# A two-layer hybrid decoder step on one core: the samples' state updates of twenty heads taken from TensorE to VectorE, and one more buffer for the first modulation weights

## The reference

```python
mod = silu(c) @ w_ada + b_ada
shift, scale, gate = split(mod, 3)
h = rmsnorm(x) * (1 + scale) + shift
cols = h @ w_in                       # q, k, v of each head, z, two gates
o = each head group's recurrence      # with a state of 128x128 per head and sample
y = x + gate * ((headnorm(o) * silu(z)) @ w_out)
```

## Time and profile before

| | us |
|---|---|
| median of three runs | 2323.64 |
| profiled execution | 2323.17 |
| its span | 2321.6 |
| TensorE busy | 2266.9 |
| VectorE busy | 1283.8 |
| ScalarE busy | 738.1 |
| POOL busy | 907.0 |

### The profile page before, as it was taken

One profiled execution on the slowest core, in us unless ns is written; L12 is line 12 of the kernel. 1 busy time (PEld: TensorE's weight loads), 2 busy tenths in 40 slices (PEclk: granted clock), 3 DMA queues, 4 the chain that ended last, 5 costly groups with the idle time before them and its releaser, 6 DMA issues.

```text
span 2321.6 us, 50275 instructions
## 1 busy us (share of the span) xinstructions
PE 2266.9 (98%) x21347; PEld 2161.7 (93%) x21347; DVE 1283.8 (55%) x2506; ACT 738.1 (32%) x1175; POOL 907.0 (39%) x668
## 2 busy tenths in 40 slices
PE   4899999999999999999999999999999999999998
PEld 3799999999999999998879999999999999999998
DVE  6346666677776344442126566567777753435444
ACT  2143322333333333421124333233333433334111
POOL 3033333333334343554333333333333443346542
PEclk9999999999999999999999999999999999999999
DMA  9952222554453333366775222244453333323332
GB/s 400 378 185 93 93 94 97 162 164 160 159 178 99 116 99 117 103 219 239 267 268 201 77 93 93 91 161 156 166 164 107 112 101 124 113 86 109 121 112 106
DMA packets 153647, 347.21 MB, mean 150 GB/s; under 512 B 14816, under 2 KB 85408, under 8 KB 127544
## 3 DMA queue, kind: packets, MB, share of 16 engines
q1 hardware_dynamic: 153424, 344.01, 43.1%
HBM read 312.07 MB, written 32.09 MB: 148 GB/s over the span
## 4 chain that ended last, share of the span: by engine, by line
PE 89%; DVE 4%; DMA 2%; DVEq 1%; POOL 1%; ACT 1%; issue 1%; SPq 0%; ACTq 0%; POOLq 0%
PE pj L685 72%; PE mx L691 3%; PE mx L1028 2%; DMA rows<-in_ada_first 1%; PE mx L1054 1%; PE mx L1042 1%; PE mx L778 1%; PE mx L744 1%; POOL wlo L653 1%; DMA spare_piece<-in_ada_first 1%; DVE t L1501 1%; PE pj L1150 1%; PE mx L1006 1%; PE mx L1056 1%; PE mx L1046 1%; PE mx L937 1%
## 5 line engine op out<-in xcount | busy, mean ns | idle before, releaser
L685 PE MATMUL pj<-hh,whi 128*128 128x260 f32 x4928 | 1418.0, 288 | 4.7 <-DVE hl L1501 3.2
L685 PE MATMUL pj<-hl,whi 128*128 128x260 f32 x4928 | 1392.8, 283 | 0.0
L685 PE MATMUL pj<-hh,wlo 128*128 128x260 f32 x4928 | 1390.6, 282 | 0.0
L653 POOL TENSOR_TENSOR wlo<-raw,whi 128x512 fp32r<-128x512 f32 x632 | 862.6, 1395 | 1323.5 <-ACT whi L1229 1323.5
L685 PEld LDWEIGHTS pj<-hh,whi 128*128 128x128 f32 x4928 | 928.1, 188 | 52.5 <-issue 46.2
L685 PEld LDWEIGHTS pj<-hl,whi 128*128 128x128 f32 x4928 | 928.5, 188 | 0.0
L685 PEld LDWEIGHTS pj<-hh,wlo 128*128 128x128 f32 x4928 | 928.0, 188 | 0.0
L1229 ACT ACTIVATE whi<-raw 128x2048 fp32r<-128x2048 f32 x158 | 302.9, 1917 | 256.8 <-PE pj L685 186.8
L1229 ACT ACTIVATE xv<-pj 128x260 f32<-128x260 f32 x188 | 64.7, 383 | 380.2 <-PE pj L685 379.9
L1501 DVE SCALAR_TENSOR_TENSOR o<-pj,mod,t 128x260 f32<-128x260 f32 (+1 forms) x56 | 24.6, 480 | 230.1 <-PE pj L685 214.5
L1229 ACT ACTIVATE t<-t 128x520 f32<-128x520 f32 (+1 forms) x126 | 79.2, 629 | 182.1 <-DVEq L1761 132.8
(11 more groups left out here) (290 smaller groups left out, 2283.3 us busy)
## 6 DMA issues: line engine op xcount, KB each, us to landing
raw<-in_w_tiles SPq DMA_DIRECT2D x128, 1024.0 KB, 4.9
raw<-in_wo_tiles SPq DMA_DIRECT2D x32, 1024.0 KB, 5.0
lev<-in_w_ada SPq DMA_DIRECT2D x90, 256.0 KB, 4.6
rows<-in_ada_first SPq DMA_DIRECT2D x22, 1024.0 KB, 21.1
lev<-in_w_ada SPq DMA_DIRECT2D x39, 512.0 KB, 5.7
out<-ss SPq DMA_DIRECT2D x32, 512.0 KB
xv<-in_w_ada SPq DMA_DIRECT2D x25, 512.0 KB, 5.8
y_kept<-o SPq DMA_DIRECT2D x2, 4160.0 KB, 17.9
```

Of the source, the lines that this page charges most:

```text
L653: last = e.tensor_tensor((wlo_third if t == 2 else wlo[:, par, :])[:, cs], w[:, cs], high_of(t)[:, cs].bitcast(F32), ALU.subtract)
L685: last = e.matmul(pj[:, 2 * par + b, 0:HALF], w[:, par, kb * P:(kb + 1) * P], x[:, kb, b * HALF:(b + 1) * HALF], start=(kb == 0 and m == 0 ...
```

## The change

- In the 20 heads that are not mLSTM (8 HGRN2, 12 retention) `sample_rows` and the four 2x256 matmuls of `states_u` are gone, as are ScalarE's copies of `apart` and `sr` and VectorE's `blocks`. Instead ScalarE issues, right after the copy of v and before the next rounding, a DMA of the samples' v (128 partitions x 8 elements) to `v_kept` in DRAM, transposed to 8 rows of 128, so element by element (`keep_v`). SP, at j = 1 of the head, waits for it and loads v_kept into `big`, the same 4 KB for all 128 partitions (512 KB). VectorE multiplies `big` by k and adds it to `ss` (`outer`, two operations of 128x1024), in HGRN2 heads before the wait for `ps["u"]`, in retention heads after "chain".
- ScalarE waits for `v_saved` before it copies vt.
- `states_u` of retention heads (but for g = 0) runs after part 3 instead of 4.
- LOW_FIRST is 2: VectorE makes two remainders of `o` ahead of `ps["u"]` and none later; POOL makes fourteen instead of twelve.
- An eleventh home for the first pieces, made of two halves: z's and zw's buffer (`z_zw`) and a new `gate_bs` that holds gate_b and gate_sum. Its piece is loaded by two DMAs of 512 KB; piece 10, its first, waits for `sq_sum`. The pieces are dealt anew (`piece_slot`), and the last ones stand in another order in TensorE's program.

```diff
@@ -282,8 +286,9 @@
         srow = rows_t[0:NS, 2 * half_h + D:2 * half_h + 2 * D]
-        piece_at = [rows_t[:, kb * TOK:kb * TOK + D] for kb in range(0, 2 * KB, 4)] + [xv[:, 0:D], spare_t[:]]
-        piece_slot = [0, 4, 1, 5, 2, 6, 3, 7, 8, 9, 1, 5, 2, 6, 3, 7, 8, 9, 2, 6, 3, 7, 8, 9, 3, 7, 8, 9, 3, 7, 8, 9]
+        piece_at = [rows_t[:, kb * TOK:kb * TOK + D] for kb in range(0, 2 * KB, 4)] + [xv[:, 0:D], spare_t[:], None]
+        halves_at = (z_zw[:, 0:D // 2], gate_bs[:])
+        piece_slot = [0, 4, 1, 5, 2, 6, 3, 7, 8, 9, 10, 1, 5, 2, 6, 3, 7, 8, 9, 10, 2, 6, 3, 7, 8, 9, 10, 3, 7, 8, 9, 10]
         yrow, ysrow = xrow, srow
...
@@ -422,7 +431,13 @@
                     e.wait_ge(piece_used, earlier[-1] + 1)
-                e.dma_start(at, ada_first[p]).then_inc(piece_in[piece_slot[p]], 16)
+                if at is None:
+                    if p == 10:
+                        e.wait_ge(sq_sum, 1)
+                    for b, half in enumerate(halves_at):
+                        e.dma_start(half, ada_first[p][:, b * D // 2:(b + 1) * D // 2]).then_inc(piece_in[piece_slot[p]], 16)
+                else:
+                    e.dma_start(at, ada_first[p]).then_inc(piece_in[piece_slot[p]], 16)
...
@@ -544,6 +559,11 @@
                             continue
+                        if j == 1 and kind != "ml":
+                            e.wait_ge(v_saved, 16 * (plain_before(g) + 1))
+                            e.wait_ge(head_done, g + 1)
+                            e.wait_ge(ps["score"], scorec(l, h, LEVELS + 1 if kind == "hg" else 1))
+                            e.dma_start(big, v_kept.rearrange("s d -> (s d)").partition_broadcast(P)).then_inc(v_in, 16)
                         if h + 1 < NH:
...
@@ -715,11 +735,14 @@
                     n, pieces = column_block(u)[2:]
-                    e.wait_ge(piece_in[piece_slot[p]], 16 * (loads_of(p) + 1))
+                    e.wait_ge(piece_in[piece_slot[p]], (32 if piece_slot[p] == 10 else 16) * (loads_of(p) + 1))
                     if i == 0 and u >= 2:
                     for x in range(FIRST_K):
-                        w = piece_at[piece_slot[p]].rearrange("p (k j n) -> p k j n", k=FIRST_K, j=4)[:, x]
+                        if piece_slot[p] == 10:
+                            w = halves_at[x // 2].rearrange("p (k j n) -> p k j n", k=FIRST_K // 2, j=4)[:, x % 2]
+                        else:
+                            w = piece_at[piece_slot[p]].rearrange("p (k j n) -> p k j n", k=FIRST_K, j=4)[:, x]
                         for j in range(4):
...
@@ -892,22 +915,22 @@
                     first_piece(24)
+                    first_piece(25)
                     third_block(6)
                     pair_block(9)
-                    first_piece(25)
                     first_piece(26)
+                    first_piece(27)
                     pair_block(10)
                     pair_block(11)
-                    first_piece(27)
                     first_piece(28)
                     first_piece(29)
+                    third_block(8)
                     first_piece(30)
-                    third_block(8)
+                    third_block(9)
                     first_piece(31)
-                    third_block(9)
                     block_columns(7)
...
@@ -992,8 +1016,10 @@
                             v_rows()
-                            k_rows()
-                            sample_rows().then_inc(ps["tr"], 1)
+                            last = k_rows()
+                            if kind == "ml":
+                                last = sample_rows()
+                            last.then_inc(ps["tr"], 1)
...
@@ -1033,17 +1059,18 @@
                             e.wait_ge(vs["a"], g + 1)
-                            e.wait_ge(vs["blk"], g + 1)
                             e.wait_ge(as_["vt"], g + 1)
                             e.wait_ge(as_["kt"], g + 1)
-                            e.wait_ge(as_["sr"], g + 1)
+                            if kind == "ml":
+                                e.wait_ge(vs["blk"], n + 1)
+                                e.wait_ge(as_["sr"], n + 1)
                             w = HD + 1 if kind == "ml" else HD
                                 last = e.matmul(mx[:, c, 0:w], kt[:, c, :], vt[:, c, 0:w], start=True, stop=True)
-                            lhs = sw if kind == "ml" else sr[:, 1, :]
-                            for j in range(4):
-                                r = slice(32 * j, 32 * j + 2)
-                                last = e.matmul(mx[:, j, 256:512], lhs[r, :], big[r, 0:256], start=True, stop=True)
+                            if kind == "ml":
+                                for j in range(4):
+                                    r = slice(32 * j, 32 * j + 2)
+                                    last = e.matmul(mx[:, j, 256:512], sw[r, :], big[r, 0:256], start=True, stop=True)
                             last.then_inc(ps["u"], 1)
...
@@ -1090,7 +1117,7 @@
                             return ({}, {}, {(2, 1): (scores, rows)}), {2: (states_u,), 4: (outputs,), 8: (back,)}
-                        return ({}, {}, {1: (scores, rows), 4: (states_u,), 7: (outputs,)}), {5: (back,)}
+                        return ({}, {}, {1: (scores, rows), 3: (states_u,), 7: (outputs,)}), {5: (back,)}
...
@@ -1353,6 +1380,8 @@
                             last.then_inc(taken, 1)
+                            if kept is not None:
+                                kept()
...
@@ -1365,19 +1394,16 @@
-                            if g:
-                                e.wait_ge(ps["tr"], g)
-                            e.wait_ge(taken, ht(g, 2))
-                            vqk = xv[:, 2 * (PAD + TOK):2 * (PAD + TOK) + 3 * TOK].rearrange("p (m t) -> p m t", m=3)[:, :, T:TOK]
-                            if scaled == "hg":
-                                act(by_four(apart[:, 1:2, :]), by_four(x1[:, PAD + T:PAD + TOK].unsqueeze(1)), ACT.Copy)
-                                last = act(by_four(apart[:, 0:3:2, :]), by_four(vqk[:, 0:3:2, :]), ACT.Copy)
+                            if scaled == "ml":
+                                e.wait_ge(taken, ht(g, 2))
+                                vqk = xv[:, 2 * (PAD + TOK):2 * (PAD + TOK) + 3 * TOK].rearrange("p (m t) -> p m t", m=3)[:, :, T:TOK]
+                                e.wait_ge(vs["qk"], g + 1)
+                                act(by_four(apart[:]), by_four(vqk), ACT.Copy).then_inc(as_["apart"], 1)
+                            e.wait_ge(ps["tr"], g + 1)
+                            if scaled == "ml":
+                                act(sr[0:GR], mx[0:GR, 3, 0:3 * HD].rearrange("p (j d) -> p j d", j=3), ACT.Copy).then_inc(as_["sr"], 1)
                             else:
-                                e.wait_ge(vs["qk"], g + 1)
-                                last = act(by_four(apart[:]), by_four(vqk), ACT.Copy)
-                            last.then_inc(as_["apart"], 1)
-                            e.wait_ge(ps["tr"], g + 1)
-                            act(sr[0:GR], mx[0:GR, 3, 0:3 * HD].rearrange("p (j d) -> p j d", j=3), ACT.Copy).then_inc(as_["sr"], 1)
+                                e.wait_ge(v_saved, 16 * (plain_before(g) + 1))
                             act(vt[:, :, 0:HD], mx[:, 1, :].rearrange("p (c d) -> p c d", c=NC), ACT.Copy).then_inc(as_["vt"], 1)
...
@@ -1387,6 +1413,13 @@
+                        def keep_v():
+
+                            e.wait_ge(taken, ht(g, 2))
+                            e.wait_ge(v_in, 16 * plain_before(g))
+                            e.dma_start(v_kept.rearrange("s d -> d s"), v[:, T:TOK],
+                                        allow_slow_non_contiguous=True).then_inc(v_saved, 16)
+
                         def log1p_exp(dst, src):
...
@@ -1409,7 +1442,7 @@
                                 take(0, x0, PAD, swapped=t3)
-                            take(2, v, 0)
+                            take(2, v, 0, kept=keep_v)
                             e.wait_ge(hc_in[g % 2], 16 * same_parity(g))
...
@@ -1881,14 +1914,12 @@
-                        e.wait_ge(as_["sr"], g + 1)
                         if kind == "ml":
+                            e.wait_ge(as_["sr"], n + 1)
                             ts(sw[0:GR], sr[0:GR, 2, :], gs[0:GR, i, 1:2], None, M)
                             blocks(sr[0:GR, 1, :], big[0:GR, 0:256])
-                        else:
-                            blocks(sr[0:GR, 2, :], big[0:GR, 0:256])
-                        e.drain().then_inc(vs["blk"], 1)
+                            e.drain().then_inc(vs["blk"], 1)
                         e.wait_ge(state_in[g % 2], (g // 2 + 1) * 16)
...
@@ -1896,7 +1927,19 @@
                         if h + 1 == NH:
-                            low_first(range(LOW_FIRST // 2))
+                            low_first(range(LOW_FIRST))
+
+                        def outer():
+
+                            e.wait_ge(v_in, 16 * (plain_before(g) + 1))
```

(40 more changed lines are left out.)

## The result

The changed kernel takes 2425.7 us (median of four runs, 2425.25 to 2427.77) beside 2323.9 of the kernel before: a ratio of 1.0436, 95% interval 1.0423 to 1.0449. It is 102 us **slower**; the prediction was 2307.9, with 2303 to 2363 as its range. The profiled execution has a span of 2423.5 us.

A forecast was written before the change was run, and what follows sets the result against it. TensorE, busy 98% of the span, was taken as the bound. Terms of -16.5 (17 heads), 0 (first head), +1.8 (last heads) and -1.1 (prologue) sum to -15.8: 2307.9 us as a median, range 2303 to 2363.

The forecast's parts named there:

- What bounds, and what is taken away: TensorE, 98% busy, bounds; three transposes (0.33 us) and L1046's matmuls (0.64) go from each non-mLSTM head: 0.97 us a head.
- X: Time from the issue of v's store to v_saved; taken as at most 5.5 us, which the retention copies allow.
- The clock: TensorE's stops: beyond the limit each microsecond of X was counted as one microsecond of stall, with no lower clock.
- slow rival: Store of v slow in all 20 heads, X = 8.5 as in the mLSTM rows: +36 us, 2360; chance 0.27.
- Y: Time from v_saved to the landing of the 512 KB broadcast; between 3.6 and 5.5 us, taken as 3.6 to 4.5.
- Y's queue: SP issues the t0+5 load behind the broadcast, 4 to 6 us later; costed at nothing, late if X grew to 9.
- VectorE in retention heads: Outer product after the chain: ss complete at 822.8, outputs want it at 824.5, so 1.7 us in hand.
- First and last heads: First head of all: gain lost, 0 (-0.8 to +1). Last head of each layer: POOL late, +1.8 us for both.
- Prologue: Loads before the first tile: one more home lets pieces issue earlier, -1.1 us (0.2 to 1.4 gained).
- the gain of the 17 heads: Heads other than the first and each layer's last, where 0.97 us a head stays whole: -16.5 us.

The follow-up runs named there:

- form 4: Kernel before plus one store a head that nobody awaits: 128 elements of 4 bytes into one full 512-byte row; landed in 7.8 to 8.5 us.
- form 0: Kernel before plus one unawaited store a head: 1024 elements of 4 bytes into 8 full 512-byte rows, as in the change; landed in 11.6 to 12.0 us.
- runs only: Changed kernel with the samples' v stored as 128 runs of 32 bytes, VectorE reading the broadcast with a stride: 2312.9 us, ratio 0.9954.
- part-4 run: Kernel with 32-byte runs, but the state update of retention heads after part 4 again instead of part 3: 2325.1 us, ratio 1.0003.
- the run with the store and its wait alone: Kernel before plus v's element-by-element store and ScalarE's wait for it, without outer product or broadcast: 2486.1 us, ratio 1.0684.
- forms 1, 2, 3 and 5: Kernel before plus an unawaited store: 128 32-byte runs; 1024 elements in 64 bytes each; 1024 in 512 each; 128 in 512 each. Executed once, 2327.3 us.

## Why the prediction was wrong, step by step

- **What bounds, and what is taken away**: right. TensorE lost 0.33 us by the transposes and 0.64 by L1046; 0.20 of the part behind L1046 was not seen. 1.17 a head instead of 0.97.
- **X, the failed step.** The prediction put both ends down, 4.6 and 8.5, and took the lower, up to 5.5, because six stores were mixed at the mLSTM tail and v's elements go to eight rows, not one. Measured: 8.4 to 10.6 us in 19 heads, 16.6 in the first. The nearer row by kind, 128 elements of 4 bytes and 6 us of tail, was the one to take: alone that form takes 7.8 to 8.5 us (form 4), and eight rows side by side do not make it cheaper (form 0).
- **The clock, a term that stood at nothing.** The prediction counted a stop of TensorE at its own length, in the slow rival too, and gave no reason. The work behind the stops took about 40 us longer at the lower clock.
- **The slow rival** had the mechanism, and for retention heads the sum: a stop of X - 5.5. In head 12 X was 10.47 and TensorE stood 5.12 us, in head 11 9.37 and 4.02. For HGRN2 heads it named the outputs only, with X + Y up to 9.9 free. That bound holds (heads 1 and 2: X + Y of 14.1 and 14.4, stops of 4.15 and 4.47), but part of each stop comes at the update already, which waits for vt there too: 16.3 us in the eight HGRN2 heads, beside 15.4 at their outputs. The rival said 2360, and 2425.7 was measured. Of the 66 us some 40 are the clock. The rest is longer stops: X 1 to 2 us above 8.5 in half of the heads, and the broadcast, Y, 5.2 us in the median where 3.6 was taken. For 3.6 no row stood; the two that the prediction names are 4.9 and 5.2.
- **Y's queue**: costed at nothing for X up to 5.5, late if X grew to 9. ScalarE did wait for a weight tile in five heads (7.6 us in the first, where it was 3.4 before, and 0.3 to 2.4 in four HGRN2 heads); TensorE stood for a weight part once, 1.3 us in the first head. With runs only the wait in the first head is left (5.2).
- **VectorE in retention heads**: the margin of 1.7 us was about right. In head 12 of the run with runs the slower strided sum ends 0.47 us before the outputs; it takes 0.97 longer than a contiguous one, so that would have had 1.4 in hand. The part-4 run shows that the earlier update was needed, there with the strided sum.
- **First and last heads**: the sign was right, the size too small. With a quick store the first head took 1.8 us longer than before where 0 was forecast, the last ones 2.4 and 5.0 where 0.9 each was.
- **Prologue**: wrong, 1.1 us forecast, none measured. The stretch behind 93.75 did carry 413 GB/s instead of 386 in the changed kernel, as hoped (371 in the run with the new prologue alone), but the last piece landed 0.4 us later than before, not earlier. Where the gain went is not shown.
- With X quick the forecast would have been 2307.9 against 2312.9 measured for the run with 32-byte runs: the first and last heads (some 7 us more than forecast) and the prologue (1.1) were taken too low, and the 0.20 a head that was not seen gives 3 back. So the gain of the 17 heads would have been nearly right, and the total near in part because errors cancel.

## What to carry to other kernels

The small stores here were not priced by their bytes nor by the number of their writes, but by how close together single elements fell. Lay a store that somebody waits for in longer runs (32 bytes were enough here), and pay with a strided read on an engine that has time. Where a new wait sits on an engine that is busy 98%, price the stop and the time at lower clock behind it: 40 us behind 82 us of stops in the changed kernel, 74 behind 89 in the run with the store and its wait alone. And where two rows bound an unknown cost, take the one of the same kind, not the one that makes the change good.

## What the runs showed of the hardware

- 128 single elements into one row of 512 bytes took 7.8 to 8.5 us from issue to landing; 1024 elements in 64 bytes each took 4.0 to 4.5, and 128 in 512 bytes each 1.4 to 3.0. In the changed kernel's head 12 the reading was over within 2 us of the issue (by 843.5), and the landings came 8 to 10.5 us behind it. This goes beyond what the Trainium skill says in "DMA: Bandwidth & Descriptors", section "Specifications", that below 512 B the transfer is a read-modify-write: forms 1, 2, 3 and 5 all write less than 512 B at a time and land in 1.4 to 6.0 us, forms 0 and 4 in 7.8 to 12.0. The measurement decides: it is the closeness of single elements that costs here.
- TensorE worked at 0.50 of its clock for about 6 us behind a stop of 5.1 us, and had a mean of 0.961 where stops before the update summed to 90.5 us.
- VectorE's 128x1024 sum with one operand read at a stride of 32 bytes took 2.45 us in the mean, 1.32 with contiguous reads. With POOL idle the times are 2.2 and 1.23; beside POOL's subtractions most are 3.0 to 3.1 and 2.17.
- What stays open: why the store-and-wait run loses nearly twice as much to the clock as the changed kernel (74 us beside 40). Its stops are fewer and longer, 20 of 4.5 us in the mean, where the changed kernel has 20 of 3.1 and 10 of 1.7. Open too: why the same store lands some 2 us later there, why form 0 with 1024 elements takes 12 us where form 4 with an eighth of them takes 8, and how far apart single elements must lie.
